# The prompt's block compression moved from the last to the first place of the key stage, in a hybrid decoder step

## What is computed

```
def nsa_compress(kv, w_ck1, w_ck2, w_cv1, w_cv2, pe_k, pe_v):
    n_chunks = N // CMP_STRIDE            # 16 tokens
    n_cmp = n_chunks - CMP_RATIO + 1      # 127 for a sample, 31 for the prompt
    ch = kv.reshape(B, n_chunks, 16, 2, NSA_KV_HEADS, HEAD_DIM)
    blocks = concatenate([ch[:, j:j + n_cmp] for j in range(2)], axis=2)
    def mlp(x, pe, w1, w2):               # x: 32 tokens x 64 -> 2048 inputs, 128 hidden
        return silu((x + pe) @ w1) @ w2
    kc, vc = mlp(blocks[..., 0], pe_k, w_ck1, w_ck2), mlp(blocks[..., 1], pe_v, w_cv1, w_cv2)
```

## Time and profile before

| | us |
|---|---|
| median of 3 runs | 1195.89 |
| the three runs | 1195.89, 1203.27, 1191.61 |
| profiled execution | 1194.02 |
| its span in the trace | 1192.2 |
| PE busy | 1084.8 (91% of the span) |
| DVE, ACT, POOL busy | 605.8, 382.4, 70.7 |
| chain that ended last | PE 64%, SP's queue 19%, issue 7%, DMA 4%, ACT 3%, DVE 3% |

### The profile page before, as it was taken

One profiled execution on the slowest core, in us unless ns is written; L12 is line 12 of the kernel. 1 busy time (PEld: TensorE's weight loads), 2 busy tenths in 40 slices (PEclk: granted clock), 3 DMA queues, 4 the chain that ended last, 5 costly groups with the idle time before them and its releaser, 6 DMA issues.

```text
span 1192.2 us, 22997 instructions
## 1 busy us (share of the span) xinstructions
PE 1084.8 (91%) x8348; PEld 951.0 (80%) x8348; DVE 605.8 (51%) x1026; ACT 382.4 (32%) x707; POOL 70.7 (6%) x83
## 2 busy tenths in 40 slices
PE   3996998988999999999999888999999999999993
PEld 2896998877888888555556557999999999999993
DVE  4331674776787782565345446445543335553332
ACT  4111112332333333545444445322231112321223
POOL 2000001111111110000000000110000000000002
PEclk9999997999899895899989998999999999999997
DMA  6529217999999942166766661323332333332221
GB/s 245 181 79 221 78 40 201 260 254 258 277 259 276 249 154 82 56 202 195 227 201 204 208 222 37 89 71 88 88 106 89 90 87 88 90 101 72 89 72 72
DMA packets 180131, 177.61 MB, mean 149 GB/s; under 512 B 13063, under 2 KB 140676, under 8 KB 177700
## 3 DMA queue, kind: packets, MB, share of 16 engines
q1 hardware_dynamic: 178610, 171.33, 50.3%
q10 hardware_dynamic: 1458, 5.43, 1.4%
HBM read 170.83 MB, written 10.06 MB: 152 GB/s over the span
## 4 chain that ended last, share of the span: by engine, by line
PE 64%; SPq 19%; issue 7%; DMA 4%; ACT 3%; DVE 3%; POOL 0%; POOLq 0%; ACTq 0%; DVEq 0%
PE bank L658 60%; SPq L572 4%; PE bank L662 4%; SPq L493 4%; SPq L532 3%; SPq L535 3%; SPq L486 2%; SPq L560 2%; DMA low_arena<-in_cache_nsa_slc_kv_dram 1%; DMA high_arena<-in_w_in_dram 1%; DMA high_arena<-in_x_sample_dram 1%; ACT low_arena L1528 1%; DMA high_arena<-in_cache_sb_kv_dram 0%; SPq L499 0%; SPq L501 0%
## 5 line engine op out<-in xcount | busy, mean ns | idle before, releaser
L658 PE MATMUL bank<-high_arena 128*128 128x254 f32 (+9 forms) x1864 | 238.7, 343 | 15.7 <-DMA high_arena<-in_cache_sb_kv_dram 6.9
L658 PEld LDWEIGHTS bank<-high_arena 128*128 128x128 f32 (+5 forms) x1864 | 185.7, 152 | 53.2 <-issue 13.5
L662 PE MATMUL bank<-low_arena 128*128 128x128 f32 (+3 forms) x658 | 104.8, 302 | 35.5 <-DMA low_arena<-in_cache_nsa_slc_kv_dram 18.0
L2083 DVE TENSOR_TENSOR w_low<-high_arena,w_high 128x1024 fp32r<-128x1024 f32 x72 | 90.1, 1251 | 85.4 <-ACT w_high L1465 73.8
L662 PEld LDWEIGHTS bank<-low_arena 128*128 128x128 f32 (+3 forms) x658 | 84.9, 160 | 46.8 <-issue 29.6
L1465 ACT ACTIVATE w_high<-high_arena 128x1024 fp32r<-128x1024 f32 x72 | 76.3, 1060 | 114.8 <-PE bank L658 113.7
L658 PE MATMUL bank<-a_high,w_high 128*128 128x256 f32 (+1 forms) x512 | 104.2, 285 | 5.3 <-issue 2.9
L658 PE MATMUL bank<-h_high,w_high 128*128 128x256 f32 (+1 forms) x512 | 103.6, 284 | 1.8 <-DVE h_low L2110 1.8
L658 PE MATMUL bank<-h_high,w_low 128*128 128x256 f32 (+1 forms) x512 | 103.8, 284 | 0.0
L658 PE MATMUL bank<-h_low,w_high 128*128 128x256 f32 (+1 forms) x512 | 103.8, 284 | 0.0
L658 PE MATMUL bank<-a_low,w_high 128*128 128x256 f32 (+1 forms) x512 | 103.7, 284 | 0.0
(11 more groups left out here) (207 smaller groups left out, 1533.8 us busy)
## 6 DMA issues: line engine op xcount, KB each, us to landing
low_arena<-in_cache_sb_kv_dram SPq DMA_DIRECT2D x128, 256.0 KB, 4.6
high_arena<-in_cache_sb_kv_dram SPq DMA_DIRECT2D x128, 256.0 KB, 3.4
high_arena<-in_cache_nsa_cmp_kv_dram SPq DMA_DIRECT2D x128, 128.0 KB, 5.0
high_arena<-in_w_up_dram SPq DMA_DIRECT2D x32, 512.0 KB, 4.0
high_arena<-in_w_down_dram SPq DMA_DIRECT2D x32, 512.0 KB, 4.2
high_arena<-in_w_in_dram SPq DMA_DIRECT2D x10, 1136.0 KB, 5.5
low_arena<-in_cache_nsa_slc_kv_dram SPq DMA_DIRECT2D x128, 64.0 KB
high_arena<-in_cache_nsa_slc_kv_dram SPq DMA_DIRECT2D x128, 64.0 KB, 2.3
```

The costliest lines, as they stand in the source:

```text
L658: return T.matmul(out, lhsT=l, rhs=r, start=start, stop=stop, **k)
L662: return T.transpose(out, in_, ident[0:n, 0:n])
L2083: V.tensor_tensor(w_lo_r[u], w_raw[u], w_hi[u], ALU.subtract).then_inc(sem(f"w_lo{u}"), 1)
```

## The change

The prompt's compression becomes the first step of the key stage on every engine. Its read-back is issued by SP ahead of the stick-breaking rows' store, behind a wait on the store of `cmp_p`, into the buffer `nat[1][0]` instead of `nat[0][0]`. The counts of the semaphores move by the prompt's steps (`past`). POOL's wait for PE's transposes of the work before, which stood in `permute`, now stands ahead of it in the samples' loop: the first half of each sample's chunks waits for the transposes of the unit before, for the first sample those of the prompt. SP's wait for `perm` ahead of a sample's compression pages counts two more.

```
             for t in range(T5):
                 sp.wait_ge(sem(f"z_ev{t}"), NCB + 1)
+            sp.wait_ge(sem("cmp_stored"), 16)
+            sp.dma_start(nat[1][0][0:2 * (NCP + 1)].rearrange("p t k h d -> p (t k h d)"),
+                O["cmp_p"][0, 0].rearrange("(c t) k h d -> c (t k h d)", t=CH // 2)).then_inc(sem("nat_in10"), 16)
             sp.dma_start(O["sb_p"][0, 0]...).then_inc(sem("sb_stored"), 16)
...
                     if ahead:
-                        sp.wait_ge(sem("perm"), i * 8 + (4 * u + half) + 1)
+                        sp.wait_ge(sem("perm"), i * 8 + (4 * u + half + 2) + 1)
                         load_chunks(page_ids(c * NPG + (NPG + 8 * half)), 1 - u, half)
...
             load_keys(3, 0, True)
-            sp.wait_ge(sem("cmp_stored"), 16)
-            sp.wait_ge(sem("perm"), 4 * 6 + 3 + 1)
-            sp.dma_start(nat[0][0][0:2 * (NCP + 1)].rearrange("p t k h d -> p (t k h d)"),
-                O["cmp_p"][0, 0].rearrange("(c t) k h d -> c (t k h d)", t=CH // 2)).then_inc(sem("nat_in00"), 16)
             load_keys(3, 1, False)
...
+            compress(0, 1, lambda: None)
             with pe.Fori(0, 4) as i:
...
                     compress(i * 2 + u, 2, lambda: todo.pop(0)())
-            compress(B, 1, lambda: None)
...
+            compress(0, 1, lambda: None)
             with Turns(chain, 4, 8) as i:
...
-            compress(B, 1, lambda: None)
             act.wait_ge(sem("kvc_ev0"), B + 1 + 1)
...
             dve.wait_ge(sem("cmp_stored"), 16)
+            silu(0, 0, NCP + 1)
+            silu(0, 1, NCP + 1)
+            compressed_out(0, kc[:, B, 0:NCP], vc[0:NCP, B, :], NCP + 1)
             with Turns(chain, 4, 2 * (NPG - 1)) as i:
...
-            silu(B, 0, NCP + 1)
-            silu(B, 1, NCP + 1)
-            compressed_out(B, kc[:, B, 0:NCP], vc[0:NCP, B, :], NCP + 1)
...
             def permute(c, kv, half, n):
-                if c:
-                    pool.wait_ge(sem(f"xT_mm{half}"), 4 * (c - 1) + 2 * kv + 2)
...
+            pool.wait_ge(sem("nat_in10"), 16)
+            for kv in range(2):
+                permute(1, kv, 0, 2 * (NCP + 1))
             for c in range(B):
                 for kv in range(2):
                     for half in range(2):
                         if kv == 0:
-                            pool.wait_ge(sem(f"nat_in{c % 2}{half}"), (c // 2 + 1) * 128)
+                            pool.wait_ge(sem(f"nat_in{c % 2}{half}"), (c // 2 + 1) * 128 + (16 if c % 2 and half == 0 else 0))
                         if c == 0 and half == 1:
                             pool.wait_ge(sem("sb_stored"), 16)
+                        if half == 0:
+                            pool.wait_ge(sem("xT_mm0"), 4 * c + 2 * kv + 2)
+                        elif c:
+                            pool.wait_ge(sem("xT_mm1"), 4 * (c - 1) + 2 * kv + 2)
                         permute(c, kv, half, P)
-            pool.wait_ge(sem("nat_in00"), 4 * 128 + 16)
-            for kv in range(2):
-                permute(B, kv, 0, 2 * (NCP + 1))
```

More of the change, by code:

```diff
@@ L773, in compress @@
                 nb = n - 1 if tiles == 2 else NCP
+                past = int(tiles == 2)
                 def chunks_T(kv, s):
@@ L778, in chunks_T @@
                         return
-                    pe.wait_ge(sem("perm"), c * 4 + (tiles * kv + half + 1) + 1)
-                    pe.wait_ge(sem(f"xT_ev{s % 2}"), c * 4 + kv * 2 + s // 2 + 1)
+                    pe.wait_ge(sem("perm"), c * 4 + (tiles * kv + half + 1 + 2 * past) + 1)
+                    pe.wait_ge(sem(f"xT_ev{half}"), c * 4 + (kv * 2 + qp + 4 * past * (1 - half)) + 1)
                     for j in range(2):
@@ L790, in hidden @@
                     if qp == 0:
-                        pe.wait_ge(sem(f"hid_ready{kv}"), c + 1)
+                        pe.wait_ge(sem(f"hid_ready{kv}"), c + past + 1)
                     for half in range(tiles):
-                        pe.wait_ge(sem(f"xT_ev{half}"), c * 4 + kv * 2 + qp + 1 + 1)
+                        pe.wait_ge(sem(f"xT_ev{half}"), c * 4 + (kv * 2 + qp + 4 * past * (1 - half)) + 1 + 1)
                     out = bank[2 + kv][:, 0:KVH * nb].rearrange("p (h c) -> p h c", h=KVH)
@@ L818, in compress @@
                 between()
-                pe.wait_ge(sem("hid_ready0"), c + 1 + 1)
-                pe.wait_ge(sem("kvc_ev0"), c + 1)
+                pe.wait_ge(sem("hid_ready0"), c + past + 1 + 1)
+                pe.wait_ge(sem("kvc_ev0"), c + past + 1)
                 for hh in range(KVH):
@@ L823, in compress @@
                 ins.then_inc(sem("w2_mm0"), 1)
-                pe.wait_ge(sem("hid_ready1"), c + 1 + 1)
-                pe.wait_ge(sem("kvc_ev1"), c + 1)
+                pe.wait_ge(sem("hid_ready1"), c + past + 1 + 1)
+                pe.wait_ge(sem("kvc_ev1"), c + past + 1)
                 for hh in range(KVH):
@@ L1296, in chunks_out @@
                         return
-                    act.wait_ge(sem(f"xT_mm{half}"), c * 4 + kv * 2 + qp + 1)
+                    act.wait_ge(sem(f"xT_mm{half}"), c * 4 + (kv * 2 + qp + 4 * past * (1 - half)) + 1)
                     m = 64 if tiles == 2 else NCP + 1
@@ L1303, in sigmoid @@
                 def sigmoid(kv):
-                    act.wait_ge(sem(f"hid_mm{kv}"), c + 1)
-                    act.wait_ge(sem(f"hid_ready{kv}"), c + 1)
+                    act.wait_ge(sem(f"hid_mm{kv}"), c + past + 1)
+                    act.wait_ge(sem(f"hid_ready{kv}"), c + past + 1)
                     e = hid[kv][:, :, 0:nb]
@@ L1714, in silu @@
                 nb = n - 1
-                dve.wait_ge(sem(f"hid_e{kv}"), c + 1)
+                past = int(n == NCH)
+                dve.wait_ge(sem(f"hid_e{kv}"), c + past + 1)
                 e = hid[kv][:, :, 0:nb]
-                dve.wait_ge(sem(f"w2_mm{kv}"), c + 1)
+                dve.wait_ge(sem(f"w2_mm{kv}"), c + past + 1)
                 hp = bank[2 + kv][:, 0:KVH * nb].rearrange("p (h c) -> p h c", h=KVH)
@@ L1722, in compressed_out @@
             def compressed_out(c, dst_k, dst_v, n):
-                dve.wait_ge(sem("w2_mm0"), c + 1 + 1)
+                past = int(n == NCH)
+                dve.wait_ge(sem("w2_mm0"), c + past + 1 + 1)
                 V.tensor_copy(dst_k, bank[4][:, 0:n - 1]).then_inc(sem("kvc_ev0"), 1)
-                dve.wait_ge(sem("w2_mm1"), c + 1 + 1)
+                dve.wait_ge(sem("w2_mm1"), c + past + 1 + 1)
                 V.tensor_copy(dst_v, bank[5][0:n - 1, 0:P]).then_inc(sem("kvc_ev1"), 1)
```

## The result

The changed kernel takes 1189.51 us (median of 20 runs, 1181.9 to 1195.26), the kernel before 1195.06 us in as many runs beside it (1188.1 to 1205.42). The ratio is 0.995, with a 95% interval of 0.9931 to 0.997: half a per cent or about 6 us faster, between 3.6 and 8.2. The forecast was 1186 in a range of 1178 to 1193. The tail went and a lag at the head took part of its place, as forecast; the gain came out smaller than the 9.8 us of the sum.

What follows compares the result with a forecast made beforehand. The prediction took the prompt's compression alone at the key stage's tail, and SP's issue pace in the middle units, as bounds: 19.1 us saved less 9.3 given back is 9.8, so 1186 us against the 1195.89 median, range 1178 to 1193.

Steps and rivals of the forecast that it cites:

- The tail: End of the key stage: the prompt's compression runs alone behind the eighth sample; moving it removes 19.1 us.
- the sum: Whole kernel: 19.1 us saved at the tail less 9.3 us of lag given back, a gain of 9.8 us.
- The head: PE ahead of the first unit: the prompt takes the same 19.39 us there, so unit work starts at 222.48, not 203.09.
- The read-back: SP's load of the prompt's rows, issued at 183.86: lands in 5 us (bounds 3.0 and 10.2), so no wait shows.
- The rival in which it comes late: Read-back landing after 201.5 delays PE's head microsecond for microsecond; beyond 211.3 the kernel is slower; chance 0.04.
- The high clock at the head: Rival: the prompt's matmuls run at 2.4 GHz at the head; gain 13 to 17 us, say 1181; chance 0.14.
- The wait that takes the tail's place: First unit: SP's third key-page group waits for PE's first key transpose; window at 237.0 against 225.39, lag 11.6 us.
- The 2.3 us recovered: Second unit: a later SP no longer meets its own waits of 2.3 us, so the lag falls from 11.6 to 9.3.
- SP's own pace sets the middle units: Units 1 to 6: SP's issuing sets 29.5 us a unit, though PE could do one in 27.58.
- PE's stalls come back in the third unit: PE's waits for key pages (18.0 us before) go in units 0 and 1, then return as SP decides again.
- The next stages move as a block: Behind the key stage: later stages start with the same instructions in the same order and shift together.
- The larger lag: Rival: narrow work leaves PE cold and the first unit stays at 1.2 GHz; gain 2 to 7 us; chance 0.12.

Runs made afterwards that it cites:

- second trace: A second profile of a kernel, unchanged: the kernel before took 1193.02 us and the changed kernel 1184.2 us, one run each.
- the two pairs: Profiles of the kernel before and the changed kernel, taken twice with both unchanged; spans 4.0 and 8.8 us shorter; the second pair's runs took 1193.02 and 1184.2 us.
- all six traces: Two traces of each kernel, one with a quarter of the prompt's first-layer matmuls (1174.97 us), one with DVE taking eight ring pages early (1189.94 us).
- half the rows: Changed kernel, but only 64 of the 128 rows of each stick-breaking key page are loaded; 1195.69 us in one run.
- paired loads: Changed kernel, but SP loads a sample's sixteen stick-breaking key pages with eight DMAs of two neighbouring fixed-place pages; 1186.88 us in one run.

## Why the prediction was right, and where it was off

*The tail.* Right: 19.1 us gone. The scores follow the eighth sample's last copy (456.74 + 0.28) by 0.1 us, with nothing else late.

*The head.* Right: 19.35 us at 0.50 instead of the 19.39 taken over from the tail, and 19.36 in the second trace.

*The read-back.* Right: 6.4 us to landing between the bounds of 3.0 and 10.2, prompt copies done at 193.65, PE there at 203.63. The rival in which it comes late did not occur.

*The high clock at the head.* Did not occur. The Trainium skill ("TensorE: Matmul & The Clock Gate", What's actually happening) calls the throttled clock the default that activity releases; here, as in the tail, 0.50 held through the whole prompt with PE busy for 17.69 of 19.35 us, so the trace again does not agree for these narrow matmuls.

*The wait that takes the tail's place.* Right in its place, and in its size at the window within the scatter: 12.2 and 8.9 us in the two pairs, for the 11.6 of the sum. What the sum took as fixed, the moment at which PE comes to the stage, was not: it lay 0.5 us later and 4.1 us earlier than in the kernel before, where the wait for the first key page hides it.

*The 2.3 us recovered.* This is the step that failed, and the term that was mis-sized: behind the window the lag did not shrink by 2.3 us but grew by 0.4 and 1.4 to the fourth unit. It is 12.7, 12.8, 10.3 and 11.3 us in the fourth and fifth unit of the two pairs, 11.8 on average, not 9.3. The prediction took SP to be late against engines that are in time. But PE and DVE are late too, and the second unit's waits moved with them: 2.8 us there after, 2.3 before. (That this is why they stayed is a reading; that the unit took its 30.9 to 32.3 us in all six traces is measured.) Put 11.8 in place of 9.3 and the sum is 19.1 - 11.8 = 7.3 us, inside the measured 3.6 to 8.2; the sum's 9.8 is outside. (The first pair's scores, 9.54 us apart, seem to confirm 9.8; the second pair's are 6.24 apart. The kernel before took 210.0 us for its seven units in the first pair and 206.5 in the second.)

PE's timeline gives the account without SP. The prompt puts 19.4 us ahead of unit 0, but unit 0 itself became shorter: from PE's start of it to its copy it took 33.9 and 33.7 us in the kernel before, with waits of 4.13 and 3.48 us for the first key page in it, and takes 28.5 and 29.2 us now. So the head hides 5.4 and 4.5 us of the prompt, and 14 to 15 of the 19 us come back as lag. With PE there 0.5 us later and 4.1 us earlier than in the kernel before, unit 0 ends 14.5 and 10.7 us later.

*SP's own pace sets the middle units.* Half right. SP slowed by 2.2 us a unit costs 2.7 (half the rows), but SP relieved of 3.4 us brings nothing (paired loads): it then waits 39.5 us for PE and DVE instead of 18.3. The forecast that PE's stalls come back in the third unit was off too: PE waits 6.7 and 10.8 us for key pages over the stage in the two traces, not 18.0, and the units are no shorter for it. PE fills the time. In the fifth unit (341.50 to 372.60) it is busy for 28.21 us at a granted clock of 0.88, waits 2.1 for a key page and 0.8 for ACT, while the eighth takes 26.00 us at 0.97. So it looks as if PE with its stretches of low clock, and SP with its fifty issues, both stand near 29 us a unit, and taking something from one finds the other. For PE this is argued and not shown: no run took work from PE in the middle units, and which share of its low stretches follows from its stalls was not taken apart.

*The next stages move as a block.* True for their order, not for their time: the time behind the scores lies between 723.8 and 736.9 us in the table, in no visible relation to the change. This scatter of 13 us is larger than the gain, which is why a single pair of traces could not size it.

*The larger lag.* The gain came out where this rival put it (2 to 7 us), but not by its mechanism, further low clock in the first unit: that unit took 27.61 us at 0.93 and, in the second trace, 28.27 at 0.91.

None of the kernels tried that do all the work beats the changed one.

## What to carry to other kernels

Work moved from the end of a pipeline to its head is hidden there only as far as the first unit had been waiting, here some 5 of 19.4 us: price it as the delay of the first unit's end on the engine that does it, and then expect the rest to follow at its own pace. A wait seen in the kernel before is only recovered by lateness if the engine waited for is not late too; ask which engines the moved work delays before subtracting it. When two resources stand within a few per cent of each other, relieving one may show nothing, so test it also by loading it more.

## What was not expected of the hardware

A DMA of 64 rows of 2 KB took 0.61 us of SP's queue (2.44 for four), one of 128 rows 0.47 (1.88 for four) with 2 KB and with 1 KB a row, and one of two pages of 128 rows about 0.51 (1.02 for two; its pages are of fixed place, not read from the page table). The DMA engines' busy share stayed at 0.94 to 1.00 when a quarter of the bytes was gone, and at 0.97 to 1.04 when the same bytes and 1024 packets of each unit were. And the same instructions at the start of the next stage ran at 0.50 and 0.86 in one execution of the changed kernel and at 0.59 and 1.00 in another.
